# The mean of squares of the recurrent heads, as two fp32r passes over a high and a low part

## The chip, the cores and the metric

One core of a Trainium2 chip runs the whole kernel. The metric is the device time of one execution in microseconds (us), the median of several runs.

## What is computed

One layer of a hybrid encoder: a combined input projection; branch A, eight heads of a gated linear recurrence (HGRN2); branch B, sliding-window attention; gates, an output projection, cross attention, a gated feed-forward part and a last norm. The change is in branch A, in the norm of each head's output `o` over its 128 values:

```
o = lax.scan(...)                       # (tokens, heads, 128)
o = o * lax.rsqrt(jnp.mean(o * o, axis=-1, keepdims=True) + EPS)
o = o * norm_g
o = o * silu(g)
```

T = 512 tokens, P = 128 values per head, 8 heads.

## The kernel before

The program is written out by hand for each engine: TensorE (PE), VectorE (DVE), ScalarE (ACT), GpSimd (POOL) and SyncE (SP) each have one list of instructions, taken in order, and semaphores (`S("name")`) with counts order them against each other. Nothing is reordered at run time, so an instruction that waits holds up all that is behind it on its engine.

Weights are in float32. Each is split into a high part in the type fp32r, which ScalarE makes by a copy (`split_hi`, L1953), and a low part, the weight less its high part, which VectorE or GpSimd makes by a subtraction (`split_lo`, L2986 and L1062). A product is then three fp32r passes on TensorE: high by low, low by high, high by high (`products`, L1189 to L1191). `chunk` runs 24 such passes of 512 columns.

The recurrent heads run as a software pipeline in `head(h, ...)`, which each engine has in its own version. In a call for `h`, TensorE makes the projections of head h in six chunks (`c` = 0 to 5) with the levels of the recurrence of head h - 1 (`level`, `turn_kh`, `states`, `outputs`) in the middle of the chunks, and the norm of head h - 2 (`tail`) at the start. `outputs` leaves `o` of a head in `bank[6]`, in the chunk c = 5 of one call; the norm follows in the next call:

- ScalarE, c = 0: the square of `bank[6]` into `osq_t` (L2160), which raises `o_squared`;
- TensorE, c = 1: a wait for `o_squared`, and the product of `ones` (128 x 128, float32) with `osq_t` into `bank[5]`, which puts the sum over the 128 values into every row (L1423), and raises `mean_done`; behind it stand level 0 of the recurrence (L1368) and the chunk c = 1;
- ScalarE, c = 1: logarithm and exponential of the mean (L2174, L2176), which give the reciprocal root `orstd_t`;
- VectorE, `tail_output`: the scaling by it, the gain and the gate (L3044, L3046).

On VectorE, `head` begins with the low part of the weights, `split_lo(0)`, then `take_level(0)` (L3026).

Calls 2 to 7 stand in a loop of three rounds with two calls in each. `head(8)` has no projection of its own: TensorE fills it with the first six chunks of the keys and values of branch B (`key_ahead`), whose low parts GpSimd makes. `head(9)` has neither projection nor recurrence, only the norm of the last head: TensorE runs `key_ahead(6)`, then the mean, then `key_ahead(7)`. On VectorE, the function `rope_angles()` (L3121 to L3132, 20 instructions, for the angles of the rotary embedding) stands between `head(8)` and `head(9)`; it waits for the end of head 8's output (`o_done`). After head 9 TensorE goes on with the chunks of branch B's queries and its attention.

Of the kernel before, what the change touches and what calls it, by code (L numbers as in the profile page):

```python
# [24 lines left out]
P = 128  # L25
D = 2048
T = 512
# [131 lines left out]
ALU = mybir.AluOpType  # L159
ACT = mybir.ActivationFunctionType  # L160
AX = mybir.AxisListType
F32 = mybir.dt.float32
F32R = mybir.dt.float32r
I32 = mybir.dt.int32
KB = 1024
# [29 lines left out]
def build_trunk(nc, a, out):  # L195

    ctx = ExitStack()
    with ctx:
        base = (nc.sbuf_base + 63) // 64 * 64

        def at(name, off, shape, dt):
            return nc.alloc_sbuf_tensor_at(name, shape, dt, offset=base + int(off))
# [3 lines left out]
        def S(name):  # L206

            if name not in sems:
                sems[name] = ctx.enter_context(nc.semaphore(name))
            return sems[name]  # L210
# [26 lines left out]
        ones = at("ones", 176.5 * KB, [P, P], F32)  # L237
# [30 lines left out]
        kh_t = at("kh_t", h_scr + 4 * KB, [P, T], F32)  # L268
        kh_nat = at("kh_nat", h_scr + 6 * KB, [P, T], F32)
        osq_t = at("osq_t", h_scr + 10 * KB, [P, T], F32)  # L270
        orstd_t = at("orstd_t", h_scr + 12 * KB, [P, T], F32)
        o1_t = at("o1_t", h_scr + 14 * KB, [P, T], F32)
        state = at("state_t", h_scr + 18 * KB, [P, NB - 1, P], F32)
# [159 lines left out]
        bank = [psum[:, i] for i in range(8)]  # L433
# [119 lines left out]
        def before(eng, semaphore, count, v=0, k=0):  # L553

            if isinstance(v, int):
                count, v = count + v * k, 0
                if count > 0:
                    eng.wait_ge(semaphore, count)
            else:
                eng.wait_ge(semaphore, v * k + count)  # L560
# [624 lines left out]
        def _(pe):  # L1185
# [164 lines left out]
            def head(h, par, project=True, mix=True, tail=True, s0=C_H, v=0, k=0, gates={}):  # L1350


                p, old = h - 1, 1 - par

                def level(l):
                    b = bank[2 + l % 2]
                    if l == 0:
                        pe.wait_ge(S("q_copied"), p + 1)
                        pe.wait_ge(S("k_ready"), p + 1)
                        if isinstance(p, int) and p == 0:  # L1360
                            pe.wait_ge(S("kv_in"), 80)
                    else:
                        pe.wait_ge(S("qk_level"), p * NL + l)
                    before(pe, S("level_taken"), l - 1, p, NL + 1)
                    if l == 0:
                        for c in range(NB):
                            f = slice(c * BLK, (c + 1) * BLK)
                            last = pe.matmul(b[:, f], k_t[:, f], q_t[:, old, f], start=True, stop=True)  # L1368
                    else:
                        for r in range(NB // 2):  # L1370
                            f = slice(r * BLK, (r + 1) * BLK)
                            last = pe.matmul(b[:, f], key_lev[:, l % 2, f], qry_lev[:, l % 2, f], start=True, stop=True)  # L1372
                    last.then_inc(S("level_done"), 1)

                def turn_kh():
                    pe.wait_ge(S("khat_ready"), p + 1)
                    before(pe, S("ln_mean"), 0, p, 1)
                    for x in range(NB):
                        f = slice(x * BLK, (x + 1) * BLK)
                        last = pe.transpose(bank[5][:, f], kh_t[:, f], ident[:, :])  # L1380
                    last.then_inc(S("kh_turned"), 1)

                def states():
                    pe.wait_ge(S("kh_nat_ready"), p + 1)
                    if isinstance(p, int):
                        pe.wait_ge(S(f"mem_in{old}"), 32 + 16 * (p // 2 + 1))
                    else:
                        pe.wait_ge(S(f"mem_in{old}"), v * 16 + (64 if par else 48))
                    before(pe, S("state_ready"), 0, p, NB - 1)
                    if isinstance(p, int) and p == 0:  # L1390
                        pe.wait_ge(S("f_staged"), NF)
                    for x in range(NB - 1):
                        f = slice(x * BLK, (x + 1) * BLK)
                        last = pe.matmul(bank[7][:, f], kh_nat[:, f], v_nat[:, old, f], start=True, stop=True)
                    last.then_inc(S("ds_done"), 1)

                def outputs():
                    pe.wait_ge(S("level_taken"), (p + 1) * (NL + 1))
                    pe.wait_ge(S("state_ready"), (p + 1) * (NB - 1))
                    pe.wait_ge(S("qe_ready"), p + 1)  # L1400
                    before(pe, S("o_scaled"), 0, p, 1)
                    for x in range(NB):
                        f = slice(x * BLK, (x + 1) * BLK)
                        last = pe.matmul(bank[6][:, f], v_nat[:, old, f], scores_a[:, f], start=True, stop=x == 0)
                        if x:
                            last = pe.matmul(bank[6][:, f], state[:, x - 1, :], qe_t[:, f], start=False, stop=True)
                    last.then_inc(S("o_done"), 1)

                def mid_chunk(c):
                    if c < 5:  # L1410
                        level(2 * (c - 1) + 1)
                    if c == 3:
                        turn_kh()
                    if c == 4:
                        states()
                    if c == 5:
                        outputs()

                for c in range(HC):
                    if c == 1 and tail:  # L1420
                        pe.wait_ge(S("o_squared"), h - 1)
                        pe.wait_ge(S("kh_nat_ready"), h - 1)
                        pe.matmul(bank[5], ones[:, :], osq_t[:, :], start=True, stop=True).then_inc(S("mean_done"), 1)  # L1423
                    if mix and 1 <= c < 5:
                        level(2 * (c - 1))
                    if mix and c and not project and c not in gates:
                        mid_chunk(c)
                    second = (lambda x=c: mid_chunk(x)) if mix and c else None
                    if c in gates:
                        if gates[c] == 0:  # L1430
                            pe.wait_ge(S("q_copied"), HEADS)
                        if gates[c] == 2:
                            pe.wait_ge(S("silu_ready"), HEADS)
                        if gates[c] in (4, 6):
                            pe.wait_ge(S("kv_kept"), gates[c] // 2 - 1)
                        key_ahead(gates[c], middle=second)
                    if project:
                        if c == 0:
                            before(pe, S("q_copied"), 0, h, 1)
                        if c == 2:  # L1440
                            before(pe, S("f_sig"), 0, h, 1)
                        if c == 4:
                            before(pe, S("silu_ready"), 0, h, 1)
                        chunk(bank[(0, 1, 4)[c // 2]], s0 + c, v, k, op_hi, op_lo, c % 2 * CK, KT, middle=second)
# [501 lines left out]
        def _(act):  # L1946
# [198 lines left out]
            def head(h, par, project=True, mix=True, tail=True, s0=C_H, v=0, k=0, gates={}):  # L2145
# [6 lines left out]
                for c in range(HC):  # L2152
# [5 lines left out]
                    if c == 0 and tail:  # L2158
                        act.wait_ge(S("o_done"), h - 1)
                        act.activation(osq_t[:, :], bank[6], ACT.Square).then_inc(S("o_squared"), 1)  # L2160
                        if not mix:
                            act.preload_act_table_set("natural_log_exp_and_others")
                            for s in range(C_S, C_S + LEAD):
                                split_hi(s)
# [594 lines left out]
        def _(dve):  # L2759
# [193 lines left out]
            def head(h, par, project=True, mix=True, tail=True, chain=True, s0=C_H, v=0, k=0):  # L2953
# [25 lines left out]
                def split_lo(c):  # L2979

                    s = s0 + c + LEAD
                    slot = s % RING
                    before(dve, w_lo_ready, s, v, k)
                    before(dve, w_hi_ready, s + 1, v, k)
                    before(dve, chunk_done, s - RING + 1, v, k)
                    dve.tensor_tensor(w_lo[:, slot], w_raw[:, slot], w_hi[:, slot].bitcast(F32), ALU.subtract).then_inc(w_lo_ready, 1)  # L2986
# [54 lines left out]
                def tail_output():  # L3041
# [3 lines left out]
                    dve.wait_ge(S("o_scaled"), h - 1)  # L3045
                    dve.scalar_tensor_tensor(o_raw[:, bass.ds(h - 2, 1), :], o1_t[:, None, :], gains[:, bass.ds(h + (G_HN - 2), 1)], silu_g[:, par:par + 1, :], ALU.mult, ALU.mult).then_inc(S("o_gated"), 1)  # L3046

                if project:
                    split_lo(0)
                if mix:  # L3050
                    take_level(0)
                if project:
# [459 lines left out]
            for u in range(XH + 1):  # L3512
                if u:
                    h = u - 1
# [335 lines left out]
```

## Time and profile before

| | us |
|---|---|
| median of 3 runs | 2682.87 |
| lowest and highest run | 2680.08 and 2684.12 |
| the profiled execution, its time | 2683.23 |
| its span, first to last instruction | 2681.4 |
| TensorE busy (matmul) | 2645.5 |
| VectorE busy | 1828.2 |
| ScalarE busy | 1374.3 |
| GpSimd busy | 531.1 |

A time line has the start of an instruction, its duration, engine, line and operation, the tiles written and read, and in brackets how long the engine had been idle before it and what ended that. Neighbours of one line are merged (x2, x4). The start of the next matmul tells how long one held TensorE: the durations of matmuls overlap.

### The profile page before, as it was taken

The page shows a single profiled execution, that of the slowest core. Times are in us where ns is not written, and L with a number is a line of the kernel's source. Part 1 is how long each engine was busy: PE and PEld are TensorE (multiplying, and loading weights), DVE is VectorE, ACT ScalarE, POOL GpSimd, SP SyncE. Part 2 cuts the span into 40 slices and gives each one's busy share as a digit, 9 for nine tenths or more (in the row PEclk, how much of TensorE's full clock was granted, in tenths as well). Part 3 has the DMA queues.
Part 4 walks back from the last instruction along what each step waited for, and adds up shares of the span by engine and source line. Part 5 has one row for each costly group of instructions (what it writes and reads, how often), then busy time and mean ns, then how long its engine had stood idle before and what let it go on. Part 6 is the DMA issues. An engine that isn't in the chain of part 4 may idle for free.

```text
span 2681.4 us, 33231 instructions
## 1 busy us (share of the span) xinstructions
PE 2645.5 (99%) x12726; PEld 2192.9 (82%) x12726; DVE 1828.2 (68%) x2124; ACT 1374.3 (51%) x1692; POOL 531.1 (20%) x382
## 2 busy tenths in 40 slices
PE   8999999999999999999999999999999999999998
PEld 7888888888888878778887888888888888888887
DVE  5865555777666788788468555666655568778788
ACT  6544444645545664545465444444444445544446
POOL 7121122000023212120241122111112212121311
PEclk9999999999999999999999999999999999999999
DMA  8887787532232399785368788787778898798975
GB/s 275 215 192 201 192 179 177 154 88 83 82 87 74 92 251 227 193 197 125 103 174 204 180 172 174 168 192 177 169 180 167 178 213 193 192 215 231 186 214 133
DMA packets 321505, 462.60 MB, mean 173 GB/s; under 512 B 30712, under 2 KB 139600, under 8 KB 318800
## 3 DMA queue, kind: packets, MB, share of 16 engines
q0 software_dynamic: 86496, 166.74, 36.2%
q1 hardware_dynamic: 231936, 288.33, 33.7%
q10 hardware_dynamic: 2928, 5.56, 0.6%
q8 instruction: 95, 1.56, 0.2%
q14 instruction: 50, 0.41, 0.0%
HBM read 426.23 MB, written 34.34 MB: 172 GB/s over the span
## 4 chain that ended last, share of the span: by engine, by line
PE 65%; DVE 5%; issue 5%; DMA 4%; POOL 1%; ACT 1%; ACTq 0%; DVEq 0%; POOLq 0%
PE psum L1189 12%; PE psum L1191 12%; PE psum L1190 12%; PE psum L1610 9%; PE psum L1612 8%; PE psum L1611 8%; DMA f_raw<-in_w_down 1%; PE psum L1372 1%; PE psum L1863 1%; DVE m_lo L3197 1%; DVE f_lo L3350 0%; DMA f_raw<-in_w_up 0%; DMA out_last<-in_w_out 0%; DMA m_tot<-in_w_proj_a 0%; DMA f_raw<-in_w_out 0%
## 5 line engine op out<-in xcount | busy, mean ns | idle before, releaser
L3571 DVE TENSOR_TENSOR f_lo<-f_raw,f_hi 128x1024 fp32r<-128x1024 f32 x458 | 559.2, 1224 | 399.8 <-ACT f_hi L2578 398.7
L2578 ACT ACTIVATE f_hi<-f_raw 128x1024 fp32r<-128x1024 f32 x460 | 486.6, 1060 | 622.3 <-PE psum L1612 306.6
L1143 POOL DMA_DIRECT2D f_raw<-in_w_up x132 | 158.9, 1204 | 662.6 <-DVE f_lo L3571 624.3
L2899 DVE TENSOR_TENSOR fr_lo<-fr_raw,fr_hi 128x1024 fp32r<-128x1024 f32 x140 | 171.3, 1225 | 158.2 <-ACT fr_hi L2027 158.0
L2027 ACT ACTIVATE fr_hi<-fr_raw 128x1024 fp32r<-128x1024 f32 x140 | 148.3, 1061 | 198.1 <-PE psum L1324 98.5
L1062 POOL TENSOR_TENSOR w_lo<-w_raw,w_hi 128x1024 fp32r<-128x1024 f32 x55 | 136.9, 2504 | 533.6 <-ACT w_hi L1953 525.4
L1189 PE MATMUL psum<-op_hi,w_lo 128*128 128x512 f32 x576 | 233.5, 405 | 0.0
L1191 PE MATMUL psum<-op_hi,w_hi 128*128 128x512 f32 x576 | 224.9, 391 | 0.0
L1190 PE MATMUL psum<-op_lo,w_hi 128*128 128x512 f32 x576 | 224.6, 390 | 0.0
L1162 POOL DMA_DIRECT2D f_raw<-in_w_down x70 | 86.1, 1454 | 285.1 <-DVE f_lo L3571 278.2
L1610 PE MATMUL psum<-f_hi,pa_lo 128*128 128x512 f32 x352 | 137.3, 390 | 1.0 <-DVE f_lo L3571 0.9
L1610 PE MATMUL psum<-f_hi,s_lo 128*128 128x512 f32 x352 | 137.0, 389 | 0.1
L1612 PE MATMUL psum<-f_hi,pa_hi 128*128 128x512 f32 x352 | 137.0, 389 | 0.0
L1611 PE MATMUL psum<-f_lo,pa_hi 128*128 128x512 f32 x352 | 137.0, 389 | 0.0
L1612 PE MATMUL psum<-f_hi,s_hi 128*128 128x512 f32 x352 | 136.9, 389 | 0.0
L1611 PE MATMUL psum<-f_lo,s_hi 128*128 128x512 f32 x352 | 136.9, 389 | 0.0
L1189 PE MATMUL psum<-f_hi,a_lo 128*128 128x512 f32 x344 | 134.8, 392 | 0.0
L1074 POOL DMA_DIRECT2D fr_raw<-in_w_in x60 | 72.4, 1207 | 311.6 <-DVE fr_lo L2899 299.0
L1191 PE MATMUL psum<-f_hi,a_hi 128*128 128x512 f32 x344 | 134.0, 390 | 0.0
L1190 PE MATMUL psum<-f_lo,a_hi 128*128 128x512 f32 x344 | 133.9, 389 | 0.0
L1191 PEld LDWEIGHTS psum<-op_hi,w_hi 128*128 128x128 f32 x576 | 108.1, 188 | 23.3
L1953 ACT ACTIVATE w_hi<-w_raw 128x1024 fp32r<-128x1024 f32 x104 | 109.1, 1055 | 31.8 <-PE psum L1191 12.6
(523 smaller groups left out, 6670.4 us busy)
## 6 DMA issues: line engine op xcount, KB each, us to landing
f_raw<-in_w_up POOLq DMA_DIRECT2D x132, 512.0 KB, 6.3
f_raw<-in_w_gate SPq DMA_DIRECT2D x88, 512.0 KB, 3.8
f_raw<-in_w_down POOLq DMA_DIRECT2D x70, 512.0 KB, 9.0
f_raw<-in_w_down SPq DMA_DIRECT2D x66, 512.0 KB, 5.3
w_raw<-in_w_in SPq DMA_DIRECT2D x64, 512.0 KB, 3.9
fr_raw<-in_w_in SPq DMA_DIRECT2D x60, 512.0 KB, 4.5
fr_raw<-in_w_in POOLq DMA_DIRECT2D x60, 512.0 KB, 7.5
f_raw<-in_w_up SPq DMA_DIRECT2D x44, 512.0 KB, 4.6
```

Of the source, the lines that this page charges most:

```text
L1062: pool.tensor_tensor(w_lo[:, slot], w_raw[:, slot], w_hi[:, slot].bitcast(F32), ALU.subtract).then_inc(w_lo_ready, 1)
L1143: pool.dma_start(raw_pieces(x, slot), up_block(n, p, c), accum_op=ALU.add).then_inc(raw_added[c], 16)
L1189: pe.matmul(b[:, 0:n], wl, xh, start=start, stop=False)
L1190: pe.matmul(b[:, 0:n], wh, xl, start=False, stop=False)
L1191: return pe.matmul(b[:, 0:n], wh, xh, start=False, stop=stop)
L1610: pe.matmul(b, lo[:, kt, f], w[0], start=False, stop=False, skip_group_check=True)
L1611: pe.matmul(b, hi[:, kt, f], w[1], start=False, stop=False, skip_group_check=True)
L1612: return pe.matmul(b, hi[:, kt, f], w[0], start=False, stop=stop, skip_group_check=True)
L2027: act.activation(fr_hi[front_slot(i)][:, :], front_source(i)[:, :], ACT.Copy).then_inc(f_hi_ready, 1)
L2578: act.activation(f_split(i)[0][:, :], split_source(i)[:, :], ACT.Copy).then_inc(f_hi_ready, 1)
L2899: dve.tensor_tensor(fr_lo[front_slot(i)][:, :], front_source(i)[:, :], fr_hi[front_slot(i)][:, :].bitcast(F32), ALU.subtract).then_inc(f_l ...
L3571: dve.tensor_tensor(lo[:, :], split_source(i)[:, :], hi[:, :].bitcast(F32), ALU.subtract).then_inc(f_lo_ready, 1)
```

## The change

The mean's product is made of two fp32r passes in place of one float32 product. ScalarE copies the squares to `osq_hi` in fp32r, VectorE subtracts that from the squares to give `osq_lo`, and TensorE multiplies `ones`, read as fp32r, with the low and then with the high part, both into `bank[5]`. The two new tiles lie at 96 KB, in a place that is free during the heads. `o_squared` now counts three steps for each head: the square, the high part, the low part. ScalarE's copy waits for its own square, VectorE's subtraction for the copy, TensorE for the subtraction. On VectorE the subtraction stands behind `split_lo(0)` and ahead of `take_level(0)`, and in `head(9)` behind all of `rope_angles()`, as the first instruction of that call.

```diff
         osq_t = at("osq_t", h_scr + 10 * KB, [P, T], F32)
+        osq_parts = at("osq_parts", 96 * KB, [P, 2, T], F32R)
+        osq_hi, osq_lo = osq_parts[:, 0], osq_parts[:, 1]
...
                     if c == 1 and tail:
-                        pe.wait_ge(S("o_squared"), h - 1)
+                        pe.wait_ge(S("o_squared"), h * 3 - 3)
                         pe.wait_ge(S("kh_nat_ready"), h - 1)
-                        pe.matmul(bank[5], ones[:, :], osq_t[:, :], start=True, stop=True).then_inc(S("mean_done"), 1)
+                        pe.matmul(bank[5], ones[:, :].bitcast(F32R), osq_lo, start=True, stop=False)
+                        pe.matmul(bank[5], ones[:, :].bitcast(F32R), osq_hi, start=False, stop=True).then_inc(S("mean_done"), 1)
...
                         act.activation(osq_t[:, :], bank[6], ACT.Square).then_inc(S("o_squared"), 1)
+                        act.wait_ge(S("o_squared"), h * 3 - 5)
+                        act.activation(osq_hi, osq_t[:, :], ACT.Copy).then_inc(S("o_squared"), 1)
...
+                def square_low():
+
+                    dve.wait_ge(S("o_squared"), h * 3 - 4)
+                    dve.tensor_tensor(osq_lo, osq_t[:, :], osq_hi.bitcast(F32), ALU.subtract).then_inc(S("o_squared"), 1)
+
                 if project:
                     split_lo(0)
+                if tail:
+                    square_low()
                 if mix:
                     take_level(0)
```

## Rows read from the trace of the kernel before

**Rows 1.** The page, busy us of TensorE, its share of the span, instructions.
```profile
PE 2645.5 (99%) x12726; PEld 2192.9 (82%) x12726; DVE 1828.2 (68%) x2124; ACT 1374.3 (51%) x1692; POOL 531.1 (20%) x382
```

**Rows 2.** Windows: stretch, its length, each engine's busy us (instructions), clock, DMA.
```profile
530.00:818.00 288.00, 288.00 (x1465) 242.82 (x1464) 197.08 (x480) 145.48 (x186) 19.45 (x8) 1.00 0.31 84
818.00:858.00 40.00, 40.00 (x240) 32.35 (x238) 21.87 (x41) 27.05 (x50) 11.87 (x6) 1.00 0.25 70
858.00:2672.50 1814.50, 1798.88 (x8599) 1486.34 (x8596) 1277.76 (x1241) 925.05 (x1154) 372.76 (x284) 1.00 0.76 181
```

**Rows 3.** Time line of TensorE in head 2, matmuls and weight load (PEld).
```profile
534.53 0.39 PE L1191 MATMUL psum<-op_hi,w_hi 128*128 128x512 f32 x1
534.53 0.41 PEld L1423 LDWEIGHTS psum<-osq_t,ones 128*128 128x128 f32 x2
534.76 1.02 PE L1423 MATMUL psum<-osq_t,ones 128*128 128x512 f32 x2
535.61 1.05 PE L1368 MATMUL psum<-q_t,k_t 128*128 128x128 f32 x8
```

**Rows 4.** Time line of ScalarE in head 2.
```profile
532.37 0.59 ACT L2160 ACTIVATE osq_t<-psum 128x512 f32<-128x512 f32 x1
...
536.27 0.67 ACT L2174 ACTIVATE orstd_t<-psum,stat 128x512 f32<-128x512 f32 x1
536.97 0.63 ACT L2176 ACTIVATE orstd_t<-orstd_t 128x512 f32<-128x512 f32 x1
```

**Rows 5.** Time line of VectorE in head 2, and a two-input instruction in head 8.
```profile
532.59 1.23 DVE L2986 TENSOR_TENSOR w_lo<-w_raw,w_hi 128x1024 fp32r<-128x1024 f32 x1 [0.34 <-ACT w_hi L1953]
...
796.81 0.68 DVE L3081 TENSOR_TENSOR qe_t<-q_t,exp_b_t 128x512 f32<-128x512 f32 x1
```

**Rows 6.** Time line of head 4, VectorE and TensorE's weight load.
```profile
613.54 1.22 DVE L2986 TENSOR_TENSOR w_lo<-w_raw,w_hi 128x1024 fp32r<-128x1024 f32 x1 [0.35 <-ACT w_hi L1953]
...
615.40 0.41 PEld L1423 LDWEIGHTS psum<-osq_t,ones 128*128 128x128 f32 x2
```

**Rows 7.** Time line of head 8: ScalarE, GpSimd, TensorE's weight load.
```profile
775.05 0.59 ACT L2160 ACTIVATE osq_t<-psum 128x512 f32<-128x512 f32 x1
775.29 2.40 POOL L1062 TENSOR_TENSOR w_lo<-w_raw,w_hi 128x1024 fp32r<-128x1024 f32 x1 [284.43 <-ACT w_hi L1953]
777.13 0.41 PEld L1423 LDWEIGHTS psum<-osq_t,ones 128*128 128x128 f32 x2
777.77 2.39 POOL L1062 TENSOR_TENSOR w_lo<-w_raw,w_hi 128x1024 fp32r<-128x1024 f32 x1
```

**Rows 8.** Time line of VectorE and GpSimd during the angles, ahead of head 9.
```profile
815.34 2.84 POOL L1062 TENSOR_TENSOR w_lo<-w_raw,w_hi 128x1024 fp32r<-128x1024 f32 x1
815.96 2.77 DVE L3130 SCALAR_TENSOR_TENSOR q_rot<-turns,q_rot 128x512 f32<-128x512 f32 x1
...
822.40 0.69 DVE L3130 SCALAR_TENSOR_TENSOR q_rot<-turns,q_rot 128x512 f32<-128x512 f32 x1
```

**Rows 9.** Time line of head 9: TensorE's weight load, VectorE's last angle and what follows.
```profile
817.56 0.41 PEld L1423 LDWEIGHTS psum<-osq_t,ones 128*128 128x128 f32 x2
...
823.58 0.43 DVE L3132 TENSOR_SCALAR turns<-q_rot 128x512 f32<-128x512 f32 x1
823.93 0.68 DVE L3044 TENSOR_TENSOR o_t<-psum,orstd_t 128x512 f32<-128x512 f32 x1
```

**Rows 10.** TensorE's time line, start, heads and end; windows (length, PE busy, clock, DMA).
```profile
7.28 3.68 PE L1224 MATMUL psum<-ident,mem_nat 128*128 128x128 f32 x16 [4.13 <-DMA mem_nat<-in_mem]
795.02 0.60 PE L1380 MATMUL psum<-ident,kh_t 128*128 128x128 f32 x4
2672.52 0.39 PE L1612 MATMUL psum<-f_hi,pa_hi 128*128 128x512 f32 x1
2676.00:2678.00 2.00, 0.00 (x0) 0.78 0.41 168
2678.00:2681.40 3.40, 0.00 (x0) 0.50 0.75 308
```

## The prediction

> **What bounds the kernel now.** I read four views in this order. First the page's busy times: TensorE works 2645.5 us of the span of 2681.4 [rows 1], so this is a TensorE kernel, and any edit counts by what it does to TensorE's stream. Second the windows of the stretch with the recurrent heads and of what follows: from 530 to 818 us TensorE is busy 288.00 of 288.00 us and from 818 to 858 us 40.00 of 40.00, while VectorE and ScalarE have room; in all the rest, 858 to 2672.5, TensorE is idle for only 1814.50 - 1798.88 = 15.6 us [rows 2]. The reader is to see that in the heads nothing makes TensorE wait. A time saved on TensorE there is therefore a time saved, and a wait put into its stream there is a time lost in full. Third the time lines around one head (they repeat every 40.4 us), where the order of the engines decides who is late. Fourth the last two heads, 8 and 9, which run outside the loop and look different.
>
> **The products.** The old mean is one fp32 product, two records: it begins at 534.76 and the next product, of line 1368, at 535.61, so it holds the stream for 0.85 us. A pass of 512 fp32r columns is the step before it, 534.53 to 534.76, 0.23 us [rows 3]. Two such passes cost 0.46 us, and 0.85 - 0.46 = 0.39 us is saved, in each of the eight heads (h = 2 to 9): 8 x 0.39 = 3.1 us. That is all that the change can give. What a page says: the Trainium skill ("FP8 and Floating Point Precision", section "TensorE Precision Notes") counts four passes for a true fp32 product; by it the old product would cost 4 x 0.23 = 0.92 us and the gain would be 3.7 us. The rows show 0.85, and the sum goes by them.
>
> **What has to be ready now.** Before, TensorE waited for ScalarE's square alone. Now it waits for the square, then a ScalarE copy (the high part), then a VectorE subtraction (the low part), and VectorE takes its instructions in the order of the program. So the question is, head by head, when VectorE reaches the subtraction.
>
> **Heads 2 to 7 (the loop).** In the first, the square runs 532.37 to 532.96. An instruction that waits for its own engine's result starts 0.03 us later (536.27 + 0.67, then 536.97), and 512 elements from SBUF to SBUF take ScalarE up to 0.63 us [rows 4]; the high part is there at 533.62. VectorE is in its split of the first weights until 532.59 + 1.23 = 533.82, and its next instruction may start some 0.08 us before that end; two SBUF inputs of 512 elements take 0.68 us [rows 5], so the low part is done at 534.42. TensorE asks for it at 534.53 [rows 3]. That just fits, with 0.11 us left; in head 4 the same count gives 613.54 + 1.22 - 0.08 + 0.68 = 615.36 against 615.40, 0.04 us left [rows 6]. A wait across engines needs a little of that, so I take 0.05 us lost in each head, 0.3 us for six; bounds 0 and 1.2 (0.2 each). VectorE pays the 0.68 us itself in a hole: next in line is the first score level, for which it waits for TensorE. ScalarE's copy pushes its next weight split and two exponentials back by 0.63 us, and of these nothing is asked for before VectorE's second split, some 3 us later. If that cover were gone it would be 0.63 us a head.
>
> **Head 8.** Here GpSimd does the weight splits. The square ends at 775.05 + 0.59 = 775.64, the high part at 776.30, and VectorE is free. But GpSimd is in a split from 775.29 to 777.69, and the next follows at 777.77 [rows 7]. What such an overlap does is seen 40 us later: the same VectorE form with two SBUF inputs takes 0.69 us alone and 2.77 us beside a GpSimd split, and it ends at 818.73, 0.55 us behind the split's end at 818.18 [rows 8]. So the low part comes at 777.69 + 0.55 = 778.24, and TensorE, which asks at 777.13, loses 1.1 us. Bounds: 0, if the subtraction isn't held up (776.30 + 0.68 is in time), and 3.6, if it comes only after the second split (780.16 + 0.55).
>
> **Head 9.** This is the big one. In VectorE's program the angles of the rotary embedding stand ahead of head 9; they end with line 3132 at 823.58, and the next instruction starts at 823.93. The subtraction takes that place: 823.93 + 0.68 = 824.61. TensorE asks for the mean at 817.56 [rows 9]. Before, it didn't need VectorE there at all and went on with a full chunk of weights; now that chunk is queued behind the mean, in order. The stall is 824.61 - 817.56 = 7.05, taken as 7.1 us. ScalarE's extra 0.63 us also moves GpSimd's two splits under the angles, which may shift VectorE's end by as much: bounds 6.5 and 7.7.
>
> **The clock behind that stall.** TensorE's granted clock is full (1.00, 2.4 GHz) until the kernel's end: the last product starts at 2672.52 and ends by 2672.91; the clock is 0.78 on average over 2676 to 2678 and 0.50 (1.2 GHz) after that. At half for (1 - 0.78) / 0.5 x 2 = 0.88 us of that stretch, it fell at 2677.1, 4.2 us after TensorE's last work. The coming 7 us without a product are longer. The price of a return: at the kernel's start, after a wait of 4.13 us for the first loads, sixteen transposes take 3.68 us, from 7.28 to 10.96, where four of the same form later take 0.60, the tail of the last one in it, so sixteen at that pace at most 2.40. I read this as the lower level of the clock, until about 11 us [rows 10]. Some 4 us at half pace lose 2.0 us. Bounds: 0 (the clock stays) and 4.0 (it returns in twice that time). The Trainium skill ("TensorE: Matmul & The Clock Gate", section "HAM oscillation — how this bites in real kernels") says the same against this change: a wait between bursts of matmuls sends the clock to half rate, and the next burst begins cold. By that rule the term is there and the sum is unchanged. If instead the clock holds through such a wait, the term is 0 and the sum 5.4.
>
> **The sum.** -3.1 (products) + 0.3 (heads 2 to 7) + 1.1 (head 8) + 7.1 (head 9) + 2.0 (clock) = +7.4 us. The profiled execution took 2683.23 us, so 2690.6; it stood 0.36 us over the median of 2682.87, and against that median the forecast is 2690.3 us, 0.28% slower. Later work gives nothing back in this sum: what follows head 9 starts from TensorE's own chunks, so VectorE and ScalarE move back with it.
>
> **The rivals.** About 0.2% (5.4 us) is what a measurement of this kernel can tell from no change.
> *The stall is absorbed (not slower).* After 858 us the chain of waits runs partly through VectorE; if its work there were the true limit, a late TensorE would find it done and win the delay back. For it: TensorE's 15.6 us of idle time [rows 2]. Against it: that idle time is spread over 1800 us in pieces behind TensorE's own products, and up to 858 there is none. All 9.1 us of stall and clock in head 9 won back leaves -3.1 + 0.3 + 1.1 = -1.7: 2681.2 us. From 2 us won back on, the result is inside 0.2%. Chance 0.10.
> *The clock stays full.* Then +5.4: 2688.3 us, right at the 0.2%. For it, that no wait of 7 us in mid-kernel is there to show the fall; against it, the two stretches of rows 10. Chance 0.12.
> *VectorE's subtraction is held up longer.* If in head 8 both splits go first (+2.5) and each head of the loop loses its 0.2 (+0.9), the sum is +10.8: 2693.7 us. For it, the 0.04 us left in head 4; against it, VectorE got in between two splits in rows 8. Chance 0.05.
> *The passes aren't cheap.* If the cast view of the ones still ran at fp32 pace, each head would cost 1.70 instead of 0.46 us: +9.9 more, 2700 us. Nothing in the profile speaks for it but that no fp32r product with these ones is there. Chance 0.03.
>
> **How the numbers follow.** The forecast has 0.70; its own range is 2688 to 2693 by the bounds of head 9 and the clock, of which some 0.10 lies under 2688.2, the line of 0.2%. The range 2686 to 2694 leaves out the absorbed stall, the fp32 pace, half of the longer hold and a little of the rest, 0.19 in all. Slower by over 0.2%: 0.60 + 0.05 (half of the full clock, roughly) + 0.05 + 0.03 = 0.73; within: 0.10 + 0.07 + 0.08 = 0.25; faster: 0.02, which would take more than the products can give.
>
> **What would show it.** Right: two records of line 1423's successor per head, 0.23 us apart; a TensorE gap of some 7 us at about 815 us (head 9), released by VectorE's subtraction, with a granted clock of 0.50 behind it and matmuls 0.43 us apart; a gap of 1 us at about 775, with the subtraction stretched to about 2 us; next to none in heads 2 to 7. Wrong: the subtraction of head 9 ahead of the angles, TensorE without a gap there, or idle time after 858 us that shrinks by as much as head 9 lost.

## The result

| | median us | runs | against before, 95% interval |
|---|---|---|---|
| before | 2682.71 | 9 | |
| changed | 2689.72 | 8 | 1.0026 [1.0017, 1.0035] |
| changed, a second time, beside other runs (before: 2682.58) | 2689.05 | 11 | 1.0023 [1.0014, 1.0032] |

A ninth run of the changed kernel took 3311.57 us at a mean granted clock of 0.752 and is left out; with it the median is 2690.14. The change makes the kernel slower, by 7.0 us and by 6.5 us in the two sets. The forecast was 2690.3 us, 7.4 us over.

The place is narrow. A useful ruler is the time between two of TensorE's products that stand on either side of heads 2 to 9: the first product of level 0 of the recurrence, which stands in call 1, just ahead of the loop (the expectations below call it the first level of the loop), and the first scores of branch B's attention. The view of one line gives the first and last start of its instructions. Of the kernel before:

```profile
L1368 PE MATMUL psum<-q_t,k_t x64: 270/275/275, 494.5 to 779.0; 128*128 128x128 f32 x64
L1465 PE MATMUL psum<-kT_pad,q_rot x256: 269/269/321, 843.3 to 941.4; 64*64 64x128 f32 x128
```

Of the changed kernel:

```profile
L1370 PE MATMUL psum<-q_t,k_t x64: 270/275/275, 495.2 to 777.9; 128*128 128x128 f32 x64
L1468 PE MATMUL psum<-kT_pad,q_rot x256: 269/269/321, 851.1 to 949.3; 64*64 64x128 f32 x128
```

That is 843.3 - 494.5 = 348.8 us before and 851.1 - 495.2 = 355.9 after: 7.1 us more between these two points, the whole difference of the medians. The 0.7 us by which the changed kernel starts later at 495 has nothing to do with the change, which begins behind it. I call this stretch the ruler below; it is steadier than the time of the whole kernel, whose runs scatter by some 2 us either way. To 2 us or so, a whole time can't tell what the ruler can.

**The loop.** The time line of head 2 in the changed kernel, which answers to [rows 3 to 5], and level 0 of head 4 (line 1370):

```profile
533.66 0.63 ACT L2165 ACTIVATE osq_parts<-osq_t 128x512 fp32r<-128x512 f32 x1
534.40 0.69 DVE L3056 TENSOR_TENSOR osq_parts<-osq_t,osq_parts 128x512 fp32r<-128x512 f32 x1
535.23 0.19 PEld L1425 LDWEIGHTS psum<-osq_parts,ones 128*128 128x128 f32 x1
535.43 0.40 PE L1425 MATMUL psum<-osq_parts,ones 128*128 128x512 f32 x1
535.66 0.39 PE L1426 MATMUL psum<-osq_parts,ones 128*128 128x512 f32 x1
535.89 1.05 PE L1370 MATMUL psum<-q_t,k_t 128*128 128x128 f32 x8
...
615.93 1.05 PE L1370 MATMUL psum<-q_t,k_t 128*128 128x128 f32 x8
```

Level 0 of head 4 in the kernel before:

```profile
616.48 1.05 PE L1368 MATMUL psum<-q_t,k_t 128*128 128x128 f32 x8
```

The two passes take 535.89 - 535.43 = 0.46 us where the float32 product took 0.85. The low part is done at 535.09 and TensorE takes it at 535.23, with no idle time before it. From level 0 of head 2 to level 0 of head 4 it is 615.93 - 535.89 = 80.04 us, and 616.48 - 535.61 = 80.87 before [rows 3]: a head takes 40.02 us instead of 40.43, 0.41 us are won in each and none of it is paid back.

**Head 8.** The time line that answers to [rows 7], from level 0 of head 7 on:

```profile
736.00 1.05 PE L1370 MATMUL psum<-q_t,k_t 128*128 128x128 f32 x8
...
773.51 5.19 POOL L1064 TENSOR_TENSOR w_lo<-w_raw,w_hi 128x1024 fp32r<-128x1024 f32 x2 [281.94 <-ACT w_hi L1956]
774.55 1.90 DVE L3056 TENSOR_TENSOR osq_parts<-osq_t,osq_parts 128x512 fp32r<-128x512 f32 x1 [1.41 <-ACT osq_parts L2165]
776.51 0.19 PEld L1425 LDWEIGHTS psum<-osq_parts,ones 128*128 128x128 f32 x1 [1.21 <-DVE osq_parts L3056]
777.08 1.06 PE L1370 MATMUL psum<-q_t,k_t 128*128 128x128 f32 x8
```

The subtraction takes 1.90 us beside GpSimd's split, not 0.69; it ends at 776.45, 0.54 us behind the end of the first of the two splits, which takes 2.40 us from 773.51 on. TensorE's weight load stands idle for 1.21 us in front of the mean. From level 0 of head 7 to that of head 8 it is 777.08 - 736.00 = 41.08 us instead of 40.02: the stream lost 1.1 us.

**Head 9.** VectorE and TensorE, which answer to [rows 8, 9], from their two time lines:

```profile
812.73 2.77 DVE L3142 SCALAR_TENSOR_TENSOR q_rot<-turns,q_rot 128x512 f32<-128x512 f32 x1
815.53 2.48 DVE L3143 TENSOR_SCALAR q_rot<-q_rot 128x512 f32<-128x512 f32 x1
...
822.41 0.43 DVE L3144 TENSOR_SCALAR turns<-q_rot 128x512 f32<-128x512 f32 x1
822.75 0.68 DVE L3056 TENSOR_TENSOR osq_parts<-osq_t,osq_parts 128x512 fp32r<-128x512 f32 x1
```

```profile
816.41 0.39 PE L1193 MATMUL psum<-op_hi,w_hi 128*128 128x512 f32 x1
823.49 0.80 PE L1425 MATMUL psum<-osq_parts,ones 128*128 128x512 f32 x1 [6.69 <-DVE osq_parts L3056]
824.08 0.63 PE L1426 MATMUL psum<-osq_parts,ones 128*128 128x512 f32 x1
824.50 0.63 PE L1191 MATMUL psum<-op_hi,w_lo 128*128 128x512 f32 x1
...
829.22 0.39 PE L1191 MATMUL psum<-op_hi,w_lo 128*128 128x512 f32 x1
...
831.95 0.39 PE L1191 MATMUL psum<-op_hi,w_lo 128*128 128x512 f32 x1
```

The low part comes right behind the last angle, TensorE's mean behind the low part, and TensorE was without work for 6.69 us (7.1 us from 816.41, where it would have loaded the ones, to 823.49, where it did). Then its passes start 0.43 us apart, later 0.23 again. The windows over that stretch, which answer to [rows 10] (length, TensorE busy, clock, DMA), show why:

```profile
816.60:821.89 5.29, 0.20 (x1) 1.00 0.66 187
821.89:823.49 1.60, 0.00 (x1) 0.50 0.00 0
823.49:828.71 5.22, 5.22 (x12) 0.50 0.01 3
828.71:832.00 3.29, 3.29 (x16) 1.00 0.00 0
```

The granted clock falls to 0.50 (1.2 GHz) while TensorE waits, and it comes back at 828.71, 5.22 us after the work did. From the mean's weight load to the next chunk it is 831.95 - 823.49 = 8.46 us; a weight load and 26 passes of 0.2275 us would be 6.14. The clock cost 2.3 us in this execution.

### The profile page after: what moved, and what is told of

Its sections match the earlier page's. It is cut to its first block, busy times and chain, and to the rows that moved or that the text cites. A ratio compares the mean times of both kernels' runs of the same rounds, so it can differ in the third digit from the quotient of the medians.

```text
span 2687.4 us, 33256 instructions
## 1 busy us (share of the span) xinstructions
PE 2646.0 (98%) x12726; PEld 2196.3 (82%) x12726; DVE 1835.1 (68%) x2132; ACT 1379.6 (51%) x1700; POOL 531.5 (20%) x382
## 4 chain that ended last, share of the span: by engine, by line
PE 66%; DVE 6%; DMA 5%; issue 3%; POOL 1%; ACT 1%; DVEq 0%; SPq 0%; ACTq 0%; POOLq 0%
PE psum L1191 11%; PE psum L1193 11%; PE psum L1192 11%; PE psum L1613 9%; PE psum L1614 9%; PE psum L1615 9%; DMA f_raw<-in_w_down 1%; PE psum L1374 1%; DMA m_low<-in_w_proj_b 1%; PE psum L1866 1%; DVE m_lo L3209 1%; DVE f_lo L3362 1%; DMA f_raw<-in_w_out 0%; DMA f_raw<-in_w_up 0%; DMA gate_b<-gate_scratch 0%
```

## The experiments

Ruler is the stretch defined above, 348.8 us before; its difference to that is given with it.

| run | ruler us | to before | median us | before beside it | ratio, 95% interval |
|---|---|---|---|---|---|
| changed | 355.9 | +7.1 | 2689.72 | 2682.71 | 1.0026 [1.0017, 1.0035] |
| changed again | 355.2 | +6.4 | 2689.05 | 2682.58 | 1.0023 [1.0014, 1.0032] |
| 1 low part among the angles | 346.5 | -2.3 | 2680.72 | 2682.82 | 0.9994 [0.9985, 1.0003] |
| 2 loop alone | 346.3 | -2.5 | 2680.18 | 2682.82 | 0.9990 [0.9980, 0.9999] |
| 3 wait filled, 29 passes | 353.5 | +4.7 | 2689.29 | 2682.82 | 1.0025 [1.0015, 1.0035] |
| 4 wait alone | 357.8 | +9.0 | 2691.97 | 2682.82 | 1.0032 [1.0020, 1.0044] |
| 5 as 1, GpSimd later | 345.3 | -3.5 | 2680.19 | 2682.58 | 0.9989 [0.9980, 0.9998] |
| 6 float32 behind the waits | 358.6 | +9.8 | 2693.06 | 2682.58 | 1.0035 [1.0022, 1.0049] |
| 7 wait filled in part, 18 passes | 355.1 | +6.3 | 2689.99 | 2682.58 | 1.0026 [1.0017, 1.0036] |
| 8 six waits, idle | 400.6 | +51.8 | 2733.62 | 2684.12 | 1.0184 [1.0167, 1.0201] |
| 9 six waits, filled | 391.0 | +42.2 | 2727.38 | 2684.12 | 1.0162 [1.0145, 1.0179] |

The changed kernel was run a second time for the runs of its set.

> The changed kernel itself, on the same chip as the next three, so that they can be held against it. About 7 us over the kernel before, 2690 us; the gap of head 9 at 7.1 us, the clock at 0.50 behind it until about 829 us.

TensorE's time line and the windows (length, TensorE busy, clock, DMA) of its profile:

```profile
816.28 0.39 PE L1193 MATMUL psum<-op_hi,w_hi 128*128 128x512 f32 x1
823.36 0.79 PE L1425 MATMUL psum<-osq_parts,ones 128*128 128x512 f32 x1 [6.68 <-DVE osq_parts L3056]
...
831.02 0.39 PE L1191 MATMUL psum<-op_hi,w_lo 128*128 128x512 f32 x1
...
820.11:823.36 3.25, 0.01 (x1) 0.50 0.18 52
823.36:826.93 3.57, 3.57 (x8) 0.50 0.00 0
```

The stall is the same, 823.36 - 816.28 = 7.08 us. The clock isn't: it fell and rose 1.8 us earlier than in the first profile, so it was at 0.50 for 3.57 us of work instead of 5.22, not until 829 as expected. From the mean's weight load to the next chunk it is 831.02 - 823.36 = 7.66 us instead of 8.46, and the clock cost 7.66 - 6.14 = 1.5 us. That is why the two rulers of one kernel differ by 0.7 us.

**1. Head 9's low part among the angles.**

```diff
                 link(dve.tensor_scalar(angle[:, :], angle[:, :], rope_cols[:, 0:1], None, ALU.mult))
+                dve.wait_ge(S("o_squared"), 23)
+                dve.tensor_tensor(osq_lo, osq_t[:, :], osq_hi.bitcast(F32), ALU.subtract).then_inc(S("o_squared"), 1)
...
-                if tail:
+                if tail and mix:
                     square_low()
```

> The changed kernel, with head 9's subtraction moved on VectorE from behind the angles to behind their third instruction; nothing else is moved. Theory (the stall of head 9 and the clock behind it are the loss): TensorE's gap of 7.1 us ahead of that mean shrinks below 0.5 us, the clock stays at 1.00 there, and of the terms there remain -3.2 (products) and +1.2 (head 8): about 2.0 us under the kernel before, some 2680.7 us. Rival (the loss is elsewhere, say in the extra copies and subtractions of every head, or in the fp32r view of the ones): still about 7 us over the kernel before. Rival (the angles, now 0.7 us later, hold up the attention behind them): gap gone, but a wait of TensorE for the rotated queries at its first scores, and a time near or over the kernel before.

VectorE's and TensorE's time lines in that run:

```profile
809.52 0.69 DVE L3137 TENSOR_TENSOR osq_parts<-osq_t,osq_parts 128x512 fp32r<-128x512 f32 x1
...
816.16 0.39 PE L1425 MATMUL psum<-osq_parts,ones 128*128 128x512 f32 x1
```

The low part is there 6 us before TensorE asks, the gap is gone, and the clock stays at 1.00 (in the window 810 to 832 us, with TensorE busy for all 22.00 of it). The same copies, subtractions and passes now take 2.1 us less than the kernel before by the medians, though the interval still holds 1, and 2.3 us less by the ruler. The ruler ends at the first scores, so these don't come late: the rival of angles that hold up the attention falls too. So the whole loss lay in the place of one instruction of 0.7 us.

**2. The loop alone.**

```diff
-                        pe.wait_ge(S("o_squared"), h * 3 - 3)
+                        pe.wait_ge(S("o_squared"), h * 3 - 3 if project else h + 11)
...
+                        if project:
+                            pe.matmul(bank[5], ones[:, :].bitcast(F32R), osq_lo, start=True, stop=False)
+                            pe.matmul(bank[5], ones[:, :].bitcast(F32R), osq_hi, start=False, stop=True).then_inc(S("mean_done"), 1)
+                        else:
+                            pe.matmul(bank[5], ones[:, :], osq_t[:, :], start=True, stop=True).then_inc(S("mean_done"), 1)
```

ScalarE's copy and VectorE's subtraction are left out in heads 8 and 9 as well.

> The change in the six heads of the loop alone; heads 8 and 9 keep the float32 product and wait for the square alone. Theory (heads 2 to 7 win 0.40 us each and wait for nothing): 2.4 us under the kernel before, some 2680.3 us, the period of a head 40.03 us instead of 40.43. Rival (each head pays part of it back in a wait for the low part): the period is 40.2 or more and the time is that of before within 0.5 us.

The ruler says 2.5 us, the medians 2.6: six times 0.4. The rival, a small wait in each head and a period of 40.2 us or more, falls: the profile shows level 0 of head 6 at 696.66 us and that of head 7 at 736.69, 40.03 us apart.

**3. The wait of head 9 filled, and 7. filled in part.**

```diff
+                        if not mix:
+                            for _ in range(29):
+                                pe.matmul(bank[1], ones[:, :].bitcast(F32R), op_hi[:, :, 0, :], start=True, stop=True)
                         pe.wait_ge(S("o_squared"), h * 3 - 3)
```

The seventh run has 18 in place of 29. The passes are extra work whose output isn't used.

> The changed kernel, with 29 fp32r passes of 512 columns into an unused bank ahead of head 9's wait, 6.6 us of work that nothing reads. Theory (a wait of that length costs twice, by its 7.1 us and by the half clock behind it): the gap is filled, the granted clock stays at 1.00, head 9's mean begins at the same place as in the changed kernel, and the matmuls behind it run at 0.23 us each: 2.3 us less than the changed kernel, about 4.8 us over the kernel before. Rival (the clock behind the gap costs nothing that isn't hidden later): the same time as the changed kernel, some 7 us over the kernel before.

> As the third experiment, but with 18 passes instead of 29, so that TensorE waits for about 2.9 us at the end of the stall instead of not at all. Theory (the clock falls only behind a long wait: 2.9 us is less than the 4.2 us after which it fell at the kernel's end): the clock stays at 1.00, the mean begins where it does in the changed kernel, from the first level of the loop to the first scores 353.5 us as with 29 passes, and in the time 2.3 us under the changed kernel. Rival 1 (any wait of some us brings it down): clock 0.50 behind the wait, 355.9 us. Rival 2 (the clock's price is won back later in the kernel): 353.5 us there, but the time of the changed kernel.

TensorE's time line with 29:

```profile
816.38 6.74 PE L1425 MATMUL psum<-op_hi,ones 128*128 128x512 f32 x29
823.25 0.50 PE L1428 MATMUL psum<-osq_parts,ones 128*128 128x512 f32 x1
...
823.82 0.39 PE L1191 MATMUL psum<-op_hi,w_lo 128*128 128x512 f32 x1
824.05 0.40 PE L1192 MATMUL psum<-op_lo,w_hi 128*128 128x512 f32 x1
816.00:832.00 16.00, 15.87 (x71) 1.00 0.23 65
```

The last line is a window (length, TensorE busy, clock, DMA). The mean begins where it did (823.25 and 823.49), and behind it the passes are 0.23 us apart at once, with the clock at 1.00. The ruler is 353.5, as the theory has it, 2.4 us and 1.7 us under the two profiles of the changed kernel. The median doesn't follow: 2689.29, where 2687.6 was expected, and nothing under the changed kernel's 2689.05. By the median this run is a miss, but its interval, 1.0015 to 1.0035 or 2686.8 to 2692.2 us, holds both numbers, so it couldn't be told from the median whether the clock's price is won back later or lies under the scatter.

With 18 passes the expectation failed in the trace. The windows (length, TensorE busy, clock, DMA):

```profile
820.60:823.30 2.70, 0.10 (x1) 1.00 0.07 22
823.30:824.64 1.34, 1.30 (x6) 1.00 0.00 0
824.64:828.05 3.41, 3.41 (x10) 0.50 0.00 0
```

TensorE was idle for 2.64 us, and the clock did fall, not in the wait but 1.3 us after the work had begun again, and for 3.41 us. The ruler is 355.1, not the expected 353.5: as long as in the second profile of the changed kernel. So a wait shorter than the 4.2 us of [rows 10] can bring the clock down too.

**4. The wait alone.** The kernel before, with float32 products, and one more line:

```diff
                         pe.wait_ge(S("o_squared"), h - 1)
+                        if not mix:
+                            pe.wait_ge(S("lb_shifted"), 1 + 2)
```

> The kernel before, float32 products and all, with one wait added: head 9's mean waits for the last of VectorE's angles. Theory (a wait put into TensorE's stream there is lost in full): a gap of 6.4 us, a half clock behind it for some 5 us of work, and 8.5 to 8.9 us over the kernel before, about 2691.4 us. Rival (later work, paced by VectorE, wins it back): 0 to 3 us over the kernel before, with idle time of TensorE behind 860 us that is smaller by the rest.

TensorE's time line shows the gap and, in the two records of the float32 product (2.05 us instead of the 1.02 of [rows 3]), the lower clock:

```profile
824.11 2.05 PE L1425 MATMUL psum<-osq_t,ones 128*128 128x512 f32 x2 [6.17 <-issue]
```

The ruler grows by 9.0 us and the median by 9.2. A single wait, with nothing else changed, costs more than the whole change did, and it is not absorbed: that rival falls. From the first scores to the last instruction the kernel takes 2692.5 - 852.4 = 1840.1 us, not less than the 2681.4 - 843.3 = 1838.1 us before.

**5. GpSimd's split behind the low part of head 8,** on top of the first experiment:

```diff
+                if s == C_KV + LEAD:
+                    pool.wait_ge(S("o_squared"), 21)
                 pool.wait_ge(w_lo_ready, s)
                 split_lo(s)
```

> The kernel of the first experiment (head 9's subtraction among the angles), with one more wait: GpSimd starts its first split of head 8 only after the low part of head 8 is made. Theory (VectorE's subtraction is held up there by GpSimd's split, and GpSimd can afford to start later): the subtraction takes 0.69 us instead of 1.90, TensorE's gap of 0.8 us (1.2 with the weight load) is gone, and from the first level of the loop to the first scores of the attention it takes 345.3 us, 1.2 less than in the first experiment and 3.5 less than before; some 2679.5 us. Rival (GpSimd's later splits come too late for TensorE's chunks): new waits for w_lo in head 8, and no gain over the first experiment.

```profile
774.20 0.69 DVE L3058 TENSOR_TENSOR osq_parts<-osq_t,osq_parts 128x512 fp32r<-128x512 f32 x1 [1.41 <-ACT osq_parts L2167]
774.97 4.87 POOL L1064 TENSOR_TENSOR w_lo<-w_raw,w_hi 128x1024 fp32r<-128x1024 f32 x2 [283.76 <-DVE osq_parts L3058]
774.97 0.19 PEld L1427 LDWEIGHTS psum<-osq_parts,ones 128*128 128x128 f32 x1
```

The time line shows the subtraction at 0.69 us and TensorE with no wait; the ruler is 1.2 us shorter than in the first experiment, to 345.3 as expected. This is the fastest of the versions by the ruler (3.5 us under before) and, with run 2, one of the two whose interval against the kernel before lies under 1: 0.9989 [0.9980, 0.9998]. Its median of 2680.19 is 2.4 us under before, where 3 us were expected; against the first experiment's 2.1 under its own before, the 1.2 us don't show.

**6. The float32 product behind all three waits.** The two passes are put back to the old product of `osq_t`; the two parts are made and not read.

> The changed kernel with all its waits, copies and subtractions, but with the mean made by the old float32 product of the squares; the two parts are made and not used. Theory (the two passes win 0.40 us a head over the float32 product, eight times, and the waits cost the same whichever product follows): 3.2 us over the changed kernel, from the first level of the loop to the first scores 359.1 us against 355.9, about 10.3 us over the kernel before. Rival (the fp32r passes win nothing, and the time follows the waits alone): the same as the changed kernel.

358.6 us by the ruler and 2693.06 by the median: 2.7 to 3.4 us over the changed kernel by the two rulers (its two profiles), 4.0 us by the medians. A stretch that the clock of head 9 doesn't touch is steadier: the view of level 0's line has it from 494.6 to 780.2 here and from 495.2 to 777.9 in the changed kernel, 285.6 us against 282.7, which is 2.9 us for the seven heads 2 to 8. So the two passes do win their 0.41 us a head, some 3.3 us in all, in the changed kernel as well; the waits took them and more.

**8 and 9. Six waits, idle and filled.** To settle what the third run left open, the price of the lower clock was put into the kernel before six times, once in each head of the loop. GpSimd, idle there, makes six subtractions of a constant tile behind the mean, and TensorE waits for them. The diff is that of the filled run, without the lines that place the constant tile and wait for it; the idle one is without the loop of 31 passes and the wait ahead of it for the last reader of their bank:

```diff
...
+            for h in range(2, 8):
+                pool.wait_ge(S("mean_done"), h - 1)
+                for j in range(6):
+                    last = pool.tensor_tensor(hold_t[:, j], scan_mask[:, :], scan_mask[:, :], ALU.subtract)
+                    last.then_inc(S("ones_set"), 1)
...
                         pe.matmul(bank[5], ones[:, :], osq_t[:, :], start=True, stop=True).then_inc(S("mean_done"), 1)
+                        if project:
+                            before(pe, S("f_sig"), 0, h, 1)
+                            for _ in range(31):
+                                pe.matmul(bank[1], ones[:, :].bitcast(F32R), op_hi[:, :, 0, :], start=True, stop=True)
+                            pe.wait_ge(S("ones_set"), h * 6 - 5)
```

> The kernel before (float32 products, one wait), with a wait of some 7 us put behind the mean of each of the six heads of the loop: GpSimd, idle there, makes six subtractions of a constant tile after the mean, and TensorE waits for the last. It asks what a wait of that length costs in the time of the whole kernel, six times over, where one is near the noise of a measurement. Theory (the wait costs its length and the half clock behind it, and nothing is won back): about 6 x (7.3 + 2.4) = 58 us over the kernel before, with the clock at 0.50 behind each wait. Rival (the clock's price is won back later in each head or in the kernel): about 44 us over.

> The same six waits with 31 fp32r passes into an unused bank in each, so that TensorE stands idle for under 1 us. Theory: the clock stays at 1.00, and the time is that of the waits alone, 6 x 7.3 = 44 us over the kernel before: some 14 us under the run with idle waits. Rival (the clock's price is won back, so filling the waits saves nothing): the same time as the run with idle waits, within 3 us.

TensorE's time line in head 2, idle:

```profile
535.25 1.02 PE L1430 MATMUL psum<-osq_t,ones 128*128 128x512 f32 x2
542.58 2.07 PE L1375 MATMUL psum<-q_t,k_t 128*128 128x128 f32 x8 [6.31 <-POOL hold_t L1088]
542.58:547.34 4.76, 4.76 (x15) 0.50 0.02 3
```

and filled:

```profile
534.85 1.02 PE L1430 MATMUL psum<-osq_t,ones 128*128 128x512 f32 x2
535.31 7.64 PE L1434 MATMUL psum<-op_hi,ones 128*128 128x512 f32 x31
542.79 1.05 PE L1375 MATMUL psum<-q_t,k_t 128*128 128x128 f32 x8
530.00:850.00 320.00, 320.00 (x1599) 1.00 0.27 74
```

The lines with two times are windows (length, TensorE busy, clock, DMA): behind the idle wait the clock was at 0.50 for 4.76 us of work, filled it stayed at 1.00. The passes turned out longer than the wait, so the difference of the two runs must be set right for that. From the mean to level 0 it takes 542.58 - 535.25 = 7.33 us idle (7.26 in the five heads that follow) and 542.79 - 534.85 = 7.94 filled, against 0.85 in the kernel before. Six delays are 6.48 + 5 x 6.41 = 38.5 us and 6 x (7.94 - 0.85) = 42.5 us. Filled, the kernel lost 42.2 us by the ruler and 43.3 by the median: the delay and nothing else. Idle, it lost 51.8 and 49.5: 13.3 and 11.0 us beyond the delay, that is 2.2 us a wait by the ruler and 1.8 by the median. The clock's price is real in the time of the whole kernel, near 2 us for each such wait. It isn't the same each time: by the starts of level 0 the six waits cost from 1.5 to 3.0 us beyond their delay. The expected 14 us between the two runs were 6.2 (medians), in part because of the longer passes; with that taken out it is 10.2, because a wait cost 1.8 us and not the 2.4 that were put in.

## Why the prediction was right, step by step

| step | forecast us | measured us | from |
|---|---|---|---|
| eight products, two fp32r passes each | -3.1 | -3.3 | eight times 0.41, the period of a head; runs 2 and 6 |
| heads 2 to 7, waits | +0.3 | 0 | period of a head; run 2 |
| head 8 | +1.1 | +1.1 | 41.08 against 40.02; run 5 |
| head 9, the stall | +7.1 | +7.1 | 816.41 to 823.49, 816.28 to 823.36; runs 1 and 4 |
| the clock behind it | +2.0 | +2.3 and +1.5 | 8.46 and 7.66 against 6.14; runs 3, 8 and 9 |
| sum | +7.4 | +7.2 and +6.4 | ruler +7.1 and +6.4, medians +7.0 and +6.5 |

The measured column has the two profiles of the changed kernel. In each the sum of the steps comes within 0.1 us of its ruler. That the forecast of 7.4 lies so near the measured 7.0 and 6.5 is in part luck: the 0.3 us for the loop were not there, the products won 0.2 us more, and the clock's price varies by 0.8 us from one execution to the next.

**The products** were right to 0.02 us a head: 0.39 by the step from product to product, 0.41 by the period. Their passes are 0.23 us apart, so the rival of fp32 pace falls.

**The loop** was tight as reckoned, and it held: run 2 shows 0.4 us won in each head. The 0.05 us a head taken for a wait across engines was not there; the chain of ScalarE's copy and VectorE's subtraction is done just in time.

**Head 8** was read from one row of an instruction that had to wait for GpSimd, 40 us later and of another kind, and it carried over: 1.90 us, ending 0.54 us after the first split (0.55 forecast), not after both. Run 5 shows that it was that split. With it and with the loop falls the rival of a longer hold. The Trainium skill ("SBUF — State Buffer", section "Who interferes with whom") has a rule for it: a VectorE instruction with two SBUF inputs contends with a GpSimd instruction that reads SBUF, and the one that comes later is blocked. The trace agrees, 0.69 us alone and 1.90 beside it. The angles show it for a second form: a TENSOR_SCALAR of 0.43 us takes 2.48 us at 815.53 beside GpSimd's second split of that place, of 814.91 to 817.73.

**Head 9** was the whole matter, and it follows from the order of the program alone: VectorE had 14 us of angles (808.70 to 822.84) in front of an instruction that TensorE came to need. Run 1 takes the stall away and run 4 makes it without the rest of the change. Some 4.1 of the 14 us are what two of the angles take longer beside GpSimd's splits, 2.77 and 2.48 us instead of 0.69 and 0.43; the forecast had them in, since it took the angles' end from the trace, and no run takes them out.

**The clock** fell, as the rows at the kernel's end had it, and cost 2.3 us in one profile and 1.5 in the other, so the rival of a full clock falls; the 2.0 us came from one stretch at the kernel's start, and runs 8 and 9 put it near 2 us a wait. The forecast lies between the two. The Trainium skill ("TensorE: Matmul & The Clock Gate", section "HAM oscillation — how this bites in real kernels") says that the burst behind a wait begins cold; the trace agrees, with a granted clock of 0.50 for the first 5.22 us. One sentence of the prediction is not borne out: it set the 7 us against the 4.2 us of [rows 10] as if that were a length that a wait has to pass. Run 7 saw the clock fall behind a wait of 2.64 us, and in the two profiles of the changed kernel, with the same wait, it fell 5.1 and 3.4 us after the last product (816.80 to 821.89, 816.67 to 820.11).

**Absorbed by later work** (the rival for no loss): run 4 loses its 9 us in full, and so do the six waits of run 9. The sign that the prediction named for it isn't there either: from the first scores to the last instruction it is 1838.1 us in the kernel before, 1836.3 and 1840.5 in the two profiles of the changed kernel, 1840.1 in run 4 and 1838.0 in run 8, with no tie to what head 9 lost. That what follows starts from TensorE's own products, the reason that the prediction gave, is read from the program and not tested by a run of its own.

**What stays open.** Filling one wait saves 1.7 to 2.4 us on the ruler but nothing that could be measured by the medians. The six waits show that such a price is in the time of the whole kernel, and in run 3's own profile it isn't won back: behind the first scores it takes 2685.6 - 848.4 = 1837.2 us, between the changed kernel's 1836.3 and 1840.5. These two numbers of one kernel differ by more than the saving, so the scatter can hide it; that it did is not shown.

## What to carry to other kernels

When an instruction gains an input from another engine, look for where that engine stands at the moment the input is asked for, at every place that the code runs and not only in the loop: six of the eight heads won 0.4 us, one lost 0.7, and the last lost 9, for one instruction in the wrong line. A wait on the engine that bounds this kernel cost its length and, on TensorE, another 1.5 to 3 us of lower clock behind it when it was 6 to 7 us long. Compare by a stretch between two products around the change when the effect is smaller than the scatter of whole runs.

## What was not expected of the hardware

The clock fell in mid-kernel behind waits of 2 us that have nothing to do with the change. In the profile of run 2 TensorE waited 2.0 us for a low part in the mixed stage, and the windows (length, TensorE busy, clock, DMA) show half the clock for 3.41 us of full work behind it:

```profile
1072.00:1082.50 10.50, 8.49 (x39) 1.00 0.78 187
1082.56:1085.97 3.41, 3.41 (x9) 0.50 0.51 172
```

In the kernel before, the same wait was 1.5 us long and the clock stayed at 1.00. The second profile of the changed kernel has such a stretch at 2421 us, behind waits of 2.4 us in all, and the profile of run 9 one at 1469 us, behind a wait of 2.1 us. These three profiles also have the longest times from the first scores to the last instruction, 1840.4 to 1841.5 us, where the other nine have 1836.3 to 1840.1. Some of the 2 us by which the runs of one kernel differ may come from such places; no run here tests that.
